# Expert stage of a one-core decoder step: token-transposed spreading inside the up product, a 20-unit weight ring, closing sums in PSUM

## The chip, the cores and the metric

The kernel runs on one core of a Trainium2 chip. The time is device time in microseconds (us) of one launch. Everything is float32. One execution was also taken by the hardware profiler; all durations below come from that one.

## What is computed

The kernel is one layer of a decoder for 256 prompt tokens and 8 sample tokens (264 rows of width 1024): sparse attention beside pooling groups, cross-attention into 256 memory tokens, and then a mixture of 32 experts, of which each token uses the 4 with the highest router score. Only that last part is changed:

```
logits  = tok @ router_w + router_b                 # (264, 32)
vals, idx = top_k(logits, 4);  gates = softmax(vals)
for each of 32 experts:
    h    = tok @ w_up[e] + b_up[e]                  # 1024 -> 2048
    gate = min(h[:, :1024], 7);  up = clip(h[:, 1024:], -7, 7)
    act  = gate * sigmoid(1.702 * gate) * (up + 1)
    acc += combine[:, e] * (act @ w_down[e] + b_down[e])   # 1024 -> 1024
y = rms_norm(h + acc) * norm_final
```

The weights of one expert are 8 MB (up) and 4 MB (down), so the 32 experts read 384 MB.

## The kernel before

**Layout.** The attention part keeps the residual h and the normalised tokens transposed, features on partitions and the 264 tokens along the row (`hT`, `xnT`: 8 blocks of 128 x 264). For the experts the kernel turns both back to tokens on partitions (`h_nat`, `xn_nat`, tiles of 128, 128 and 8 tokens; the `hn` transposes, L957, and the multiplication at L1687).

**One expert** works on 64 slots. VectorE writes a 0/1 matrix `slot_of` that says which token sits in which slot (`assign_slots`, L1740 to L1746). TensorE then does, in this order (`expert`, from L1035 on):

1. up product: 8 chunks (`unit(0..7)`, 1 MB each: 128 rows of 8 KB), four matmuls of 512 columns a chunk, in pairs side by side in two column halves of the array (L1042), into the banks `psh0`, `psh1`;
2. `gather_tokens` for the next expert (L1006): `slot_of` times `xn_nat`, two tiles of 128 tokens and one of 8, into `psx`;
3. `spread_rows` of the previous expert's output (L1029), in three parts r = 0, 1, 2, one a token tile: the turned slot matrix `ST` times `outb`, two matmuls of 512 columns, side by side in two row halves. VectorE adds each part, times the gate, into `h_nat` (L1754); a part waits until the part before is added (`y_added`);
4. between those parts: three transposes of the slot matrix (L1052), `up_bias` for the next expert (L1016, four matmuls with 32 rows), the four transposes of the gathered tokens (L1023) and of the activations (L1063);
5. down product: 4 chunks (`unit(8..11)`), L1075, into `pso`.

When the up product is full, VectorE clips gate and up (L1762, L1763), multiplies (L1766), ScalarE has computed the sigmoid (L1303), and VectorE multiplies again (L1769); when the down product is full it copies it to `outb` (L1780). ScalarE copies PSUM to SBUF for the transposes (L1283, L1287, L1306, L1309).

**Weights.** SyncE's queue issues all weight loads, in program order (L494 up, L499 down). There are 12 units of 1 MB. Chunk c of expert n+1 is loaded as soon as chunk c of expert n has been read (`chunk_free`). Before expert 0, the 12 chunks of expert 0 are loaded: 8 when cross-attention has freed their memory, 4 after the `mo` product. All queues are in order, and every engine counts semaphores; nothing is planned at run time but the list of experts, which the router part writes (two experts to a loop iteration).

**End.** After the last expert, three more `spread_rows`, each waiting for VectorE's add; then for each token tile ScalarE squares and sums (L1318) and takes the root (L1321), VectorE normalises (L1801), and SyncE stores.

Of the kernel before, what the change touches and what calls it, by code (L numbers as in the profile page):

```python
# [18 lines left out]
ALU = mybir.AluOpType  # L19
ACT = mybir.ActivationFunctionType  # L20
F32 = mybir.dt.float32
# [38 lines left out]
def shape_constants():  # L60
# [47 lines left out]
    c["iota64"] = np.tile(p % 64, (P, 1))  # L108
# [37 lines left out]
def psum_jobs():  # L146
# [44 lines left out]
    js += [("hn", r, g) for r in range(3) for g in range(2)]  # L191
    js += [("rsn",), ("rl",), ("pos",), ("gT",), ("item",)]
# [3 lines left out]
def build(nc, ins, outs, consts, ybuf):  # L196
# [6 lines left out]
    with ExitStack() as ctx:  # L203
# [61 lines left out]
        group_at["late"] = top[0]  # L265
        UT = misc(4, 16 + NT)
        assert width["late"] <= 4 * (16 + NT)
# [13 lines left out]
        un = at(temp_off + 2 * NT, 512)  # L281
        QB = misc(TS, 32)
# [9 lines left out]
        top8 = misc(8)  # L292
        vflat = misc(512)
        pnew = misc(2, P)
        stat = misc(64)
# [38 lines left out]
        u12 = 12 * UNIT  # L334
        h_nat = at(u12, 3, D)
        xn_nat = at(u12 + 3072, 3, D)
        gain_ffn = at(u12 + 6144, D)
        gain_fin = at(u12 + 7168, D)
        xe = at(u12 + 8192, 512)
        xeT = at(u12 + 8704, 4, P)  # L340
        actT = at(u12 + 9216, 4, P)
        gate_b = at(u12 + 9728, 512)
        sig_b = at(u12 + 10240, 512)
        act_b = at(u12 + 10752, 512)
        outb = at(u12 + 11264, 512)
        slot_of = [at(u12 + 11776, 3, P), at(qT_off, 3, P)]
        ST = [at(qT_off + 384, 3 * P), at(qT_off + 768, 3 * P)]
        ysq = at(4 * UNIT, 3, D)
        ybias = at(qiT_off, D)
        esel = [at(qiT_off + 1024, SLOTS), at(qiT_off + 1088, SLOTS)]  # L350
        posb = at(qiT_off + 1152, 3)
        gsc = at(qiT_off + 1156, 3)
        meta = at(qiT_off + 1160, 3, 2, NE)
        base = at(qiT_off + 1352, LIST)
        item_x = at(qiT_off + 1416, LIST)
        item_e = at(qiT_off + 1480, LIST).bitcast(I32)
        n_items = at(qiT_off + 1544, 1).bitcast(I32)
        n_pairs = at(qiT_off + 1545, 1).bitcast(I32)
        cur = [at(qiT_off + 1546, 3), at(qiT_off + 1549, 3)]
# [11 lines left out]

        pw_sb = misc(4, P)
        rw_sb = misc(KD, NE)
        rb_sb = misc(NE)

        banks = [ctx.enter_context(nc.psum_tensor(f"bank{b}", [P, 512], F32)) for b in range(8)]
# [70 lines left out]
        def _(sp):  # L447
# [31 lines left out]
            for g in range(4):  # L479
                wait_drained(sp, "pw", g)  # L480
# [6 lines left out]
            load(gain_ffn, norm_ffn.to_broadcast([P, D]), "gain_ffn_in")  # L487
            load(gain_fin, norm_final.rearrange("(o d) -> o d", o=1).to_broadcast([P, D]), "gain_fin_in")

            def load_expert(e, chunk):  # L490
                u = unit(chunk, UNIT)
                if chunk < 8:
                    src = w_up[0, bass.ds(e, 1), chunk * P:(chunk + 1) * P, :].rearrange("o p n -> p (o n)")
                    sp.dma_start(u, src).then_inc(S(f"chunk{chunk}_in"), 16)  # L494
                else:
                    j = chunk - 8
                    src = w_down[0, bass.ds(e, 1), 2 * j * P:2 * (j + 1) * P, :].rearrange(
                        "o (k p) n -> p (o k) n", p=P)
                    sp.dma_start(u.rearrange("p (k n) -> p k n", k=2), src).then_inc(S(f"chunk{chunk}_in"), 16)  # L499

            for chunk in range(4, 12):
                load_expert(0, chunk)
            wait_filled(sp, "mo", 7)
            for chunk in range(4):
                load_expert(0, chunk)
# [6 lines left out]
            def chunk_free(chunk, n):  # L512

                if chunk == 7:
                    sp.wait_ge(S("up_full"), n + 1)
                elif chunk == 11:
                    sp.wait_ge(S("down_full"), n + 1)
                else:
                    sp.wait_ge(S("chunk_read"), n * 10 + (chunk + 1 if chunk < 7 else chunk))

            for chunk in range(12):
                chunk_free(chunk, 0)
                load_expert(1, chunk)
            sp.wait_ge(S("list_ready"), 3)

            pairs = sp.value_load(n_pairs[0:1, :], min_val=NE // 2, max_val=LIST // 2 - 2)
            with sp.Fori(0, pairs - 1) as j:
                for b in range(2):
                    e = sp.value_load(item_e[0:1, bass.ds(j * 2 + 2 + b, 1)], min_val=0, max_val=NE - 1)
                    for chunk in range(12):  # L530
                        chunk_free(chunk, j * 2 + 1 + b)
                        load_expert(e, chunk)

            for r in range(3):
                sp.wait_ge(S("y_ready"), r + 1)
                dst = y_prompt[0, r * P:(r + 1) * P, :] if r < 2 else y_sample.rearrange("b s d -> (b s) d")
                sp.dma_start(dst, h_nat[0:ROWS[r], r, :]).then_inc(S("stored_y"), 16)
# [5 lines left out]
        def _(pool):  # L543
# [33 lines left out]
            for b in range(2):  # L577
                pool.memset(ST[b], 0.0).then_inc(S("st_zero"), 1)
# [6 lines left out]
        def _(pe):  # L585
# [366 lines left out]
            for r in range(3):  # L952
                for g in range(2):
                    b = take(pe, "hn", r, g)
                    for i in range(4):
                        k = 4 * g + i
                        ins = pe.transpose(b[0:ROWS[r], i * P:(i + 1) * P], hT[:, k, r * P:r * P + ROWS[r]], ident)  # L957
                    done(ins, "hn", r, g)
            b = take(pe, "rsn")
            pe.wait_ge(S("rstd_ready"), 3)  # L960
            for r in range(3):
                ins = pe.transpose(b[0:ROWS[r], r * P:(r + 1) * P], temp[:, 2, r * P:r * P + ROWS[r]], ident)
            done(ins, "rsn")
# [7 lines left out]
            done(ins, "rl")  # L971

# [27 lines left out]
            def gather_tokens(b, nth):  # L1000

                pe.wait_ge(S("slots_ready"), nth)
                for r in range(3):
                    w = ROWS[r]
                    for o in range(2):
                        ins = pe.matmul(psx[64 * o:64 * o + 64, :], slot_of[b][0:w, r, 64 * o:64 * o + 64],  # L1006
                                        xn_nat[0:w, r, o * 512:(o + 1) * 512], start=(r == 0), stop=(r == 2),
                                        skip_group_check=True)
                ins.then_inc(S("xe_full"), 1)

            def up_bias(b):

                for o in range(2):
                    for g, ps in enumerate((psh0, psh1)):
                        rows = slice(32 + 32 * g, 64 + 32 * g)
                        pe.matmul(ps[64 * o:64 * o + 64, :], esel[b][rows, :], ybias[rows, o * 512:(o + 1) * 512],  # L1016
                                  start=True, stop=False, skip_group_check=True)

# [7 lines left out]
            def spread_rows(b, r):  # L1026

                for o, ps in enumerate((psy0, psy1)):
                    ins = pe.matmul(ps[:, :], ST[b][64 * o:64 * o + 64, r * P:(r + 1) * P], outb[64 * o:64 * o + 64, :],  # L1029
                                    start=True, stop=True)  # L1030
                ins.then_inc(S("y_full"), 1)

# [801 lines left out]
```

## Time and profile before

| | us |
|---|---|
| three runs | 1430.21, 1431.46, 1432.88 (median 1431.46) |
| the profiled execution | 1439.72 |
| its span, first to last instruction | 1437.5 |
| TensorE busy | 1282.2 (89%) |
| VectorE busy | 486.9 (34%) |
| ScalarE busy | 213.7 (15%) |
| memory read in the span | 449.24 MB |

Busy times overlap between engines. The chain is the sequence of work, each piece released by the one before, that ended last. A row `64*128 64x512` is a matmul with 64 rows of the array, 128 columns of it, and 512 columns streamed; a float32 matmul leaves two records in the trace.

### The profile page before, as it was taken

The numbers are of one execution on the slowest core, as the hardware profiler recorded it, in microseconds if no ns is written. First come the engines' busy times: TensorE is split into PE (matmuls) and PEld (weight loads), VectorE is DVE, ScalarE is ACT, GpSimd is POOL, SyncE is SP. The second block draws the span as 40 slices with busy tenths as digits, with TensorE's granted clock in tenths as the row PEclk, the third lists the DMA queues.
The fourth block names the chain that finished last, engine by engine and source line by source line (L and its number), as shares of the span: only waits on it lengthen the run. The fifth ranks groups of instructions, "written<-read, shape, count | busy, mean of one in ns | idle before, by whom it ended". The sixth has DMA issues, their size and how long they took to land.

```text
span 1437.5 us, 16965 instructions
## 1 busy us (share of the span) xinstructions
PE 1282.2 (89%) x6251; PEld 572.7 (40%) x6251; DVE 486.9 (34%) x1057; ACT 213.7 (15%) x387; POOL 39.4 (3%) x46
## 2 busy tenths in 40 slices
PE   5997663897967999999999999999999999999996
PEld 3864532885652333333333333333333333333331
DVE  2358358202343322233322233322333222332224
ACT  2124231101321101011010111101111010110102
POOL 1012400000000000000000000000000000000000
PEclk9999775589977999999999999999999999999997
DMA  9303430333274999999999999999999999999980
GB/s 377 98 23 146 170 123 1 118 125 117 99 293 188 375 403 417 415 414 417 412 415 413 414 417 414 414 412 414 415 416 415 412 417 411 417 414 413 415 357 30
DMA packets 88088, 451.99 MB, mean 314 GB/s; under 512 B 8540, under 2 KB 9080, under 8 KB 53751
## 3 DMA queue, kind: packets, MB, share of 16 engines
q1 hardware_dynamic: 85631, 437.76, 75.3%
q0 software_dynamic: 2432, 13.89, 2.6%
q8 instruction: 17, 0.28, 0.1%
q14 instruction: 8, 0.07, 0.0%
HBM read 449.24 MB, written 2.61 MB: 314 GB/s over the span
## 4 chain that ended last, share of the span: by engine, by line
PE 82%; DVE 11%; issue 3%; ACT 2%; DMA 1%; POOL 1%; another core or an unknown queue 0%; SPq 0%; DVEq 0%; ACTq 0%
PE bank L1042 31%; PE bank L1075 16%; PE bank L1029 8%; PE bank L1006 6%; PE bank L629 4%; PE bank L1016 2%; PE bank L859 2%; DVE mem L1754 2%; PE bank L844 2%; PE bank L1023 1%; DVE mem L1555 1%; PE bank L868 1%; PE bank L1052 1%; PE bank L948 1%; PE bank L608 1%
## 5 line engine op out<-in xcount | busy, mean ns | idle before, releaser
L1042 PE MATMUL bank<-mem 128*64 128x512 f32 x2048 | 446.6, 594 | 0.8 <-ACT mem L1287 0.8
L1042 PEld LDWEIGHTS bank<-mem 128*64 128x64 f32 x2048 | 147.7, 137 | 293.8 <-issue 293.8
L1075 PE MATMUL bank<-mem 128*64 128x512 f32 x1024 | 226.8, 595 | 0.0
L1754 DVE SCALAR_TENSOR_TENSOR mem<-bank,mem 128x512 f32<-128x512 f32 (+1 forms) x198 | 139.1, 742 | 132.8 <-PE bank L1029 132.8
L1762 DVE TENSOR_SCALAR mem<-bank 128x512 f32<-128x512 f32 x32 | 22.1, 692 | 425.7 <-PE bank L1042 425.7
L1029 PE MATMUL bank<-mem 64*128 64x512 f32 x396 | 113.7, 651 | 33.4 <-DVE mem L1754 32.6
L1075 PEld LDWEIGHTS bank<-mem 128*64 128x64 f32 x1024 | 70.8, 137 | 152.1 <-issue 152.1
L1303 ACT ACTIVATE mem<-mem 128x512 f32<-128x512 f32 x32 | 20.2, 631 | 706.7 <-DVE mem L1762 706.7
L1006 PE MATMUL bank<-mem 128*64 128x512 f32 (+1 forms) x396 | 97.2, 609 | 2.5 <-DVE mem L1746 2.5
L1104 ACT ACTIVATE mem<-bank 128x512 f32<-128x512 f32 (+8 forms) x119 | 59.9, 530 | 189.1 <-PE bank L629 55.2
L1029 PEld LDWEIGHTS bank<-mem 64*128 64x128 f32 x396 | 30.2, 187 | 75.6 <-DVE mem L1754 42.6
L629 PE MATMUL bank<-mem 128*128 128x264 f32 (+1 forms) x224 | 53.9, 398 | 6.3 <-DVE mem L1343 6.3
L1780 DVE COPY mem<-bank 128x512 f32<-128x512 f32 x32 | 22.1, 692 | 95.6 <-PE bank L1075 95.6
L1006 PEld LDWEIGHTS bank<-mem 128*64 128x64 f32 (+1 forms) x396 | 25.6, 136 | 68.0 <-issue 68.0
L629 PEld LDWEIGHTS bank<-mem 128*128 128x128 f32 (+1 forms) x224 | 42.5, 191 | 16.2 <-DVE mem L1343 6.5
L712 PE MATMUL bank<-mem 128*128 128x128 f32 x128 | 21.9, 346 | 17.3 <-POOL mem L566 8.1
L1016 PE MATMUL bank<-mem 32*64 32x512 f32 x264 | 35.9, 613 | 0.0
L859 PE MATMUL bank<-mem 128*128 128x264 f32 x128 | 31.6, 413 | 0.5 <-DVE mem L1602 0.5
L859 PEld LDWEIGHTS bank<-mem 128*128 128x128 f32 x128 | 26.2, 206 | 5.6 <-DVE mem L1602 0.6
L844 PE MATMUL bank<-mem 128*64 128x8 f32 x256 | 27.4, 249 | 0.9 <-DVE mem L1597 0.9
L712 PEld LDWEIGHTS bank<-mem 128*128 128x128 f32 x128 | 20.2, 184 | 19.1 <-issue 8.8
L687 PE MATMUL bank<-mem 128*128 128x512 f32 x64 | 27.7, 594 | 0.0
(293 smaller groups left out, 943.5 us busy)
## 6 DMA issues: line engine op xcount, KB each, us to landing
mem<-in_w_up_dram SPq DMA_DIRECT2D x256, 1024.0 KB, 12.3
mem<-in_w_down_dram SPq DMA_DIRECT2D x128, 1024.0 KB, 7.7
mem<-in_w_in_dram SPq DMA_DIRECT2D x8, 868.0 KB, 19.0
mem<-in_w_o_dram SPq DMA_DIRECT2D x1, 4096.0 KB, 12.8
mem<-in_cache_mem_k_dram SPq DMA_DIRECT2D x1, 4096.0 KB, 15.5
mem<-in_cache_mem_v_dram SPq DMA_DIRECT2D x1, 4096.0 KB, 15.6
mem<-in_w_mk_dram SPq DMA_DIRECT2D x1, 2048.0 KB, 29.3
mem<-in_w_mv_dram SPq DMA_DIRECT2D x1, 2048.0 KB, 35.6
```

The lines of the kernel that those rows point to most:

```text
L629: ins = pe.matmul(b[0:w, 0:NT], w_in_sb[k][:, m * P:m * P + w], xnT[:, k, :], start=(k == 0), stop=(k == KD - 1))
L687: ins = pe.matmul(b[:, :], memT[:, k, t * P:(t + 1) * P], w[:, k, :], start=(k == 0), stop=(k == KD - 1))
L712: ins = pe.transpose(b[:, j * P:(j + 1) * P], both[:, (4 * i + j) % 32, :], ident)
L844: pe.matmul(o, V2[:, n * NPG + pg, :], spT[:, s, pg, 32 * b4:32 * b4 + NH], start=(pg == 0), stop=False)
L859: ins = pe.matmul(b[:, 0:NT], w_o_sb[:, k, m * P:(m + 1) * P], mixT[:, k, :], start=(k == 0), stop=(k == KD - 1))
L1006: ins = pe.matmul(psx[64 * o:64 * o + 64, :], slot_of[b][0:w, r, 64 * o:64 * o + 64], xn_nat[0:w, r, o * 512:(o + 1) * 512], start=(r == 0 ...
L1016: pe.matmul(ps[64 * o:64 * o + 64, :], esel[b][rows, :], ybias[rows, o * 512:(o + 1) * 512], start=True, stop=False, skip_group_check=True)
L1029: ins = pe.matmul(ps[:, :], ST[b][64 * o:64 * o + 64, r * P:(r + 1) * P], outb[64 * o:64 * o + 64, :], start=True, stop=True)
L1042: ins = pe.matmul(ps[64 * o:64 * o + 64, :], lhs, w[:, g * 1024 + o * 512:g * 1024 + (o + 1) * 512], start=False, stop=(k == 7), skip_grou ...
L1075: ins = pe.matmul(pso[64 * o:64 * o + 64, :], lhs, w[:, kk, o * 512:(o + 1) * 512], start=(k == 0), stop=(k == 7), skip_group_check=True)
L1104: ins = act.activation(out, in_, ACT.Copy)
L1754: ins = dve.scalar_tensor_tensor(out=v, in0=ps[0:w, :], scalar=gsc[0:w, r:r + 1], in1=v, op0=ALU.mult, op1=ALU.add)
```

## The change

- The output of an expert is spread with tokens along the row: `outb` is the stationary operand and `ST` (64 slots x 264 tokens a half) streams. Four parts c = 0..3, each two matmuls of 264 columns for two blocks of 128 features, are put between the up product's chunks (after chunks 0, 1, 2 and 4). VectorE adds them into `hT`. The gate is already in `ST`: `gate_slots` writes slot matrix times gate (`gated`), and that is transposed.
- `h_nat`, the `hn` and `rsn` transposes and the multiplication at L1687 go. The normalised tokens are turned from `xnT` (`xr`, 24 transposes after the router product).
- 20 units: the up chunks have two sets (chunk c of experts n and n+2 share a unit), the down chunks one. Before the loop, all of expert 0 and the eight up chunks of expert 1 are loaded (14 chunks where 8 were issued at first, then 4 and 1, and 1 after the `xr` transposes). A chunk stays 128 rows of 8 KB (up).
- `gather_tokens` is split: the two tiles of 128 tokens after the up product, the 8 samples together with the biases. The gate half of the up product releases VectorE before the up half is complete (`gate_full`), and sigmoid times gate is computed first.
- The last two experts stand outside the loop. The last one multiplies `hT` by the identity into PSUM (`turn_residual`, 8 matmuls a token tile), its output is spread on top of that, and ScalarE and VectorE read the sums from PSUM.

```diff
-            def expert(b, n):
-                pe.wait_ge(S("xet_copied"), n + 1)
-                for k in range(8):
-                    ...
-                gather_tokens(1 - b, n + 2)
-                pe.wait_ge(S("rows_out"), n + 1)
-                pe.wait_ge(S("st_copied"), n + 1)
-                spread_rows(1 - b, 0)
-                ...
-                up_bias(1 - b)
-                turn_tokens(n + 2)
-                pe.wait_ge(S("y_added"), n * 3 + 1)
-                spread_rows(1 - b, 1)
-                ...
-                spread_rows(1 - b, 2)
+            def spread_rows(c):
+                for o, ps in enumerate((psy0, psy1)):
+                    ins = pe.matmul(ps[:, 0:NT], outb[64 * o:64 * o + 64, c * P:(c + 1) * P],
+                                    ST[64 * o:64 * o + 64, :], start=True, stop=True)
+                ins.then_inc(S("y_full"), 1)
+            def up_product(b, n):
+                pe.wait_ge(S("xet_copied"), n + 1)
+                for chunk in range(8):
+                    up_chunk(b, n, chunk)
+                    if chunk == 0:
+                        pe.wait_ge(S("rows_out"), n + 1)
+                        pe.wait_ge(S("st_copied"), n + 1)
+                        spread_rows(0)
+                    elif chunk in (1, 2, 4):
+                        c = (1, 2, 4).index(chunk) + 1
+                        pe.wait_ge(S("y_added"), n * 4 + c)
+                        spread_rows(c)
+            def expert(b, n):
+                up_product(b, n)
+                gather_prompts(n + 2)
+                pe.wait_ge(S("act_ready"), n + 1)
+                pe.wait_ge(S("st_copied"), n + 1)
+                turn_activations()
+                gather_samples_and_bias()
+                pe.wait_ge(S("actt_copied"), n + 1)
+                down_chunk(n, 0)
+                turn_tokens(n + 2)
+                down_chunk(n, 1)
+                turn_slots()
+                down_chunk(n, 2)
+                down_chunk(n, 3)
+            def last_expert(b, n):
+                up_product(b, n)
+                pe.wait_ge(S("act_ready"), n + 1)
+                turn_activations()
+                pe.wait_ge(S("y_added"), n * 4 + 4)
+                turn_residual(0)
+                pe.wait_ge(S("actt_copied"), n + 1)
+                down_chunk(n, 0)
+                turn_slots()
+                turn_residual(1)
+                down_chunk(n, 1)
+                turn_residual(2)
+                down_chunk(n, 2)
+                down_chunk(n, 3)
 ...
-            with sp.Fori(0, pairs - 1) as j:
+            with sp.Fori(0, loops) as j:
                 for b in range(2):
-                    e = ...item_e[j * 2 + 2 + b]
+                    e_up = ...item_e[j * 2 + 2 + b];  e_down = ...item_e[j * 2 + 1 + b]
                     for chunk in range(12):
-                        chunk_free(chunk, j * 2 + 1 + b)
-                        load_expert(e, chunk)
+                        chunk_read(chunk, j * 2 + b)
+                        load_expert(b, e_up if chunk < 8 else e_down, chunk)
```

## Rows read from the trace of the kernel before

**Rows 1.** The page: busy us (share of span, instructions); GB/s in 40 slices.
```profile
PE 1282.2 (89%) x6251; PEld 572.7 (40%) x6251; DVE 486.9 (34%) x1057; ACT 213.7 (15%) x387; POOL 39.4 (3%) x46
GB/s 377 98 23 146 170 123 1 118 125 117 99 293 188 375 403 417 415 414 417 412 415 413 414 417 414 414 412 414 415 416 415 412 417 411 417 414 413 415 357 30
```
**Rows 2.** The chain over one expert: start us, us, what, pieces.
```profile
508.45 13.73 PE bank L1042 x64
522.18 2.72 PE bank L1006 x12
524.90 1.06 PE bank L1029 x4
525.96 0.52 PE bank L1052 x3
526.49 1.02 PE bank L1016 x8
527.50 0.58 PE bank L1023 x4
528.09 1.08 PE bank L1029 x4
...
529.25 0.61 issue
529.87 0.75 DVE mem L1754
530.66 1.13 PE bank L1029 x4
531.79 7.02 PE bank L1075 x32
538.81 13.73 PE bank L1042 x64
```
**Rows 3.** Timeline after an up product: start, us, engine line op [idle before].
```profile
825.84 0.69 DVE L1762 TENSOR_SCALAR mem<-bank 128x512 f32<-128x512 f32 x1 [13.04 <-PE bank L1042]
826.57 0.63 ACT L1303 ACTIVATE mem<-mem 128x512 f32<-128x512 f32 x1 [21.64 <-DVE mem L1762]
827.97 0.69 DVE L1769 TENSOR_TENSOR mem<-mem 128x512 f32<-128x512 f32 x1
```
**Rows 4.** Timeline before expert 0: samples' gather and biases, second records.
```profile
443.10 0.59 PE L1006 MATMUL bank<-mem 8*64 8x512 f32 x2
443.11 0.61 PE L1016 MATMUL bank<-mem 32*64 32x512 f32 x4
```
**Rows 5.** Groups by line, 384 to 446 us: busy us, mean ns, idle before.
```profile
L948 PE MATMUL bank<-mem 128*128 128x264 f32 x64 | 14.5, 387 | 0.8 <-DVE mem L1652 0.8
```
**Rows 6.** Up chunks issued at 522.36, 552.72, 1190.31, 1220.66: KB, us to landing.
```profile
mem<-in_w_up_dram SPq DMA_DIRECT2D x1, 1024.0 KB, 15.1
mem<-in_w_up_dram SPq DMA_DIRECT2D x1, 1024.0 KB, 14.9
mem<-in_w_up_dram SPq DMA_DIRECT2D x1, 1024.0 KB, 14.8
mem<-in_w_up_dram SPq DMA_DIRECT2D x1, 1024.0 KB, 15.5
```
**Rows 7.** The chain at the start of expert 0.
```profile
445.81 15.65 PE bank L1042 x64
```
**Rows 8.** Timeline: first issues of expert 1's chunks, and VectorE's token multiplication.
```profile
449.39 12.44 SPq L494 DMA_DIRECT2D mem<-in_w_up_dram  x8
425.27 3.67 DVE L1687 SCALAR_TENSOR_TENSOR mem<-mem 128x1024 f32<-128x1024 f32 x3
```
**Rows 9.** Timeline of the end of the kernel.
```profile
1419.33 0.69 DVE L1780 COPY mem<-bank 128x512 f32<-128x512 f32 x1 [2.98 <-PE bank L1075]
1430.36 1.28 DVE L1801 SCALAR_TENSOR_TENSOR mem<-mem 128x1024 f32<-128x1024 f32 x1
1433.97 1.27 DVE L1801 SCALAR_TENSOR_TENSOR mem<-mem 8x1024 f32<-8x1024 f32 x1
```

More of the change, by code:

```diff
@@ L971, in _ @@
             done(ins, "rl")
+            for r in range(3):
+                for g in range(2):
+                    b = take(pe, "xr", r, g)
+                    for i in range(4):
+                        k = 4 * g + i
+                        ins = pe.transpose(b[0:ROWS[r], i * P:(i + 1) * P], xnT[:, k, r * P:r * P + ROWS[r]], ident)
+                    done(ins, "xr", r, g)
             b = take(pe, "pos")
@@ new lines, in up_chunk @@
+            def up_chunk(b, n, chunk):
+                pe.wait_ge(S(f"up{chunk}_in{b}"), n * 8 + (16 - 8 * b))
+                w = ring(b, chunk)
+                k = chunk
+                lhs = xeT[:, k % 4, 64 * (k // 4):64 * (k // 4) + 64]
+                for g, ps in enumerate((psh0, psh1)):
+                    for o in range(2):
+                        ins = pe.matmul(ps[64 * o:64 * o + 64, :], lhs, w[:, g * 1024 + o * 512:g * 1024 + (o + 1) * 512],
+                                        start=False, stop=(k == 7), skip_group_check=True)
+                    if k == 7 and g == 0:
+                        ins.then_inc(S("gate_full"), 1)
+                ins.then_inc(S("chunk_read" if k < 7 else "up_full"), 1)
@@ new lines, in _ @@
+            last_expert(1, loops * 2 + 1)
+            pe.wait_ge(S("rows_out"), loops * 2 + 3)
+            pe.wait_ge(S("st_copied"), loops * 2 + 3)
+            for ps, r in tiles:
+                w = ROWS[r]
+                for o in range(2):
+                    ins = pe.matmul(ps[0:w, o * 512:(o + 1) * 512], ST[64 * o:64 * o + 64, r * P:r * P + w],
+                                    outb[64 * o:64 * o + 64, :], start=False, stop=True, skip_group_check=True)
+                ins.then_inc(S("y_sum"), 1)
@@ new lines, in add_rows, with expert @@
+            def add_rows(n, c):
+                dve.wait_ge(S("y_full"), n * 4 + c + 1)
+                v = hT.rearrange("p (o c) t -> p c o t", o=2)[:, c]
+                ps = psum[:, 6 * 512:8 * 512].rearrange("p (o t) -> p o t", o=2)[:, :, 0:NT]
+                dve.tensor_tensor(v, v, ps, ALU.add).then_inc(S("y_added"), 1)
+            def expert(n, last):
+                if not last:
+                    e = dve.value_load(item_e[0:1, bass.ds(n + 2, 1)], min_val=0, max_val=NE - 1)
+                for c in range(4):
+                    add_rows(n, c)
+                dve.wait_ge(S("gate_full"), n + 1)
+                dve.tensor_scalar(gate_b, banks[3], 7.0, None, ALU.min).then_inc(S("gate_ready"), 1)
@@ L1779, in expert @@
+                if not last:
+                    dve.wait_ge(S("st_full"), n + 1)
+                    dve.wait_ge(S("xe_full"), n + 2)
+                    gate_slots()
+                    dve.wait_ge(S("gated_ready"), n + 2)
+                    assign_slots(n + 3, e)
                 dve.wait_ge(S("down_full"), n + 1)
-                dve.tensor_copy(outb, banks[5][:, :]).then_inc(S("rows_out"), 1)
+                dve.tensor_copy(outb, banks[5]).then_inc(S("rows_out"), 1)
             dve.wait_ge(S("list_ready"), 3)
-            dve.memset(gate_b, 0.0).then_inc(S("rows_out"), 1)
```

362 lines of the change are left out of this document (167 added, 195 removed).

## The prediction

> **What bounds the kernel now.** I read the page's busy shares and 40 slices first, then the chain of waits, then the timeline of one expert, then the landings of the weight loads. The page [rows 1] shows two resources near their limit for the whole second half: TensorE (89% of the span) and the DMA engines, which move 412 to 417 GB/s in slice after slice; VectorE (34%) and ScalarE (15%) are far from it. Which of the two sets the pace the chain says [rows 2]: from one up product to the next it runs 538.81 − 508.45 = 30.36 us, and it is TensorE work but for one hole, 0.61 + 0.75 us, where the last `spread_rows` part waits for VectorE to add the part before. No piece of it is a transfer. So the loop is bound by TensorE, with about 1 us of waiting in it.
>
> The DMA is only just behind. The last up chunk of one expert, issued at 522.36, landed after 15.1 us, at 537.5; the one an expert later at 552.72 + 14.9 = 567.6 [rows 6]. That is 30.1 us for 12 chunks, with work always queued: a chunk costs 2.51 us. Now and then it stumbles: 1190.31 + 14.8 = 1205.1 and 1220.66 + 15.5 = 1236.2 are 31.1 us apart. I count four such expert periods, of about 1 us extra each, in the 31 (near 630, 800, 1010 and 1220 us), so the DMA's own period is 30.1 + 4/31 ≈ 30.25 us. TensorE's 30.36 hides it with 0.1 us to spare. Whatever is taken out of TensorE's expert beyond that has to be carried by chunks that are already loaded, and the change loads 8 more before expert 0.
>
> **TensorE's time for one expert after the change.** From [rows 2], piece by piece.
> - Up product 13.73: 64 records, two side by side, so 32 steps of 0.429. Unchanged.
> - Four spreads. Today two matmuls of 512 columns take 1.06, where two steps are 0.86: 0.2 is the switch to another tile shape, weights in view and the last records running out. The down product after it takes 7.02 where 16 steps are 6.86, so a switch back costs about 0.05 plus the run-out 0.09. For 264 columns a step is 14.5/64 = 0.226 [rows 5]; two are 0.45. Each spread between two up chunks is then 0.09 + 0.10 + 0.45 + 0.09 + 0.05 = 0.77, four 3.1. Bounds: 0.45 each (nothing shown of a switch, 1.8 in all), and 1.2 each (today's 1.06 with 512 columns plus the way back, 4.8). I take 0.77, since every switch in rows 2 has that size.
> - `gather_prompts`: 4 of the 6 steps that fill 2.72, 1.72.
> - Wait for the activations. Today VectorE begins 0.2 after TensorE has passed on (825.84 against 825.62, where this expert's gather starts) and ends at 828.66, 3.0 after it [rows 3]. Now the gate half is released two steps (0.86) earlier: gate clip at −0.64 to 0.05, sigmoid (0.63) to 0.7, up clip 0.22 to 0.9, two multiplications of 0.69 to 2.35. TensorE resumes at 2.4, 0.6 after its gather has ended. Behind this new wait stand the activation transposes, biases and the down product; nothing else uses TensorE.
> - Activation transposes 0.58, as L1023.
> - Biases with samples. Before expert 0 the samples' gather and the biases have their second records at 443.10 and 443.11 [rows 4]: six matmuls side by side, in the time of four. So 1.02 + 0.05 for all; bounds 1.07 and 1.07 + 0.86 if they follow each other. I take 1.07, the very same instructions.
> - Down product 6.86 + 0.05, with token transposes (0.58 + 0.14) and slot transposes (0.52 + 0.14) inside: 8.3.
>
> Sum: 13.73 + 3.1 + 2.4 + 0.58 + 1.07 + 8.3 = 29.2 us, 1.2 below today. Bounds: 27.9 and 31.7.
>
> The Trainium skill speaks against the four insertions: *TensorEngine Tiling (Array Packing)*, section Tiling Modes, says that a change of tiling mode, not just of tile, drains TensorE. The trace agrees, about 0.2 us for going into a shape and 0.14 for leaving it. Counted in the order of the code, an expert goes from 9 changes of shape to 15.
>
> The covers: `rows_out` for spread 0 is ready 0.23 + 0.69 after the down product [rows 9], inside chunk 0's 1.72. Each add, about 0.75, has at least one whole chunk between two spreads (1.72, then 1.72, then 3.43). ScalarE's copies lie under biases and down chunks, 0.6 each. VectorE's slot work (2 to 3 us) starts when the slot transposes are done and has the 3.5 us of the last two down chunks; it would delay `outb` only if it took 1 us more. These I cost at nothing.
>
> **The DMA against it.** Let T be the start of expert 0. All 12 chunks of expert 0 and 8 of expert 1 are there. The first issue of the loop follows the first chunk read, T + 3.6 (449.39 − 445.81 [rows 7, 8], TensorE's clock being low there). 8 chunks occupy the DMA to T + 23.7; the first down unit comes free at T + 15.65 + 3.1 + 4.1 + 1.8 = T + 24.6, so 0.9 is lost once. From then on a queue is always there, and group k (8 up of expert k+2, 4 down of expert k+1) ends at T + 4.5 + 30.25(k+1), landing 2.4 later.
> TensorE's need: expert k+1's first down chunk at T + 1.9 + 29.2(k+1) + 16.8 + 4.1, where 1.9 is 15.65 − 13.73. It lands at T + 4.5 + 30.25k + 9 × 2.51 + 2.4. The reserve is 22.5 − 1.05k, about 1 less for the fourth down chunk: used up near k = 20. So I expect no wait for weights in the first twenty experts, at 29.2 each, and then PE held to 30.25 by the down chunks.
> The last landing before the end is that of expert 30's fourth down chunk: T + 4.5 + 907.5 + 2.4 = T + 914.4. TensorE then has that chunk's 1.7 and the last expert: up 16.8, wait 2.4, transposes 0.6, residual 2.3, down chunk 1.8, slots 0.7, residual 2.3, chunk 1.7, residual 2.3, two chunks 3.5 = 34.4. A residual part is 8 matmuls, 16 records, at 0.145 each (0.58/4, L1023). The down product ends at D = T + 950.5.
> By TensorE alone D would be T + 1.9 + 31 × 29.2 + 34.4 = T + 941.5. The later one holds; they meet at 29.5 us an expert.
>
> **The ends.** Before: D = 1419.1 = T + 973.3, and 18.4 us follow. After: copy to `outb` at D + 0.2, spreads at D + 1.0, ScalarE at D + 2.2, first normalisation at D + 4.2; the three are (1433.97 − 1430.36)/2 = 1.8 apart [rows 9]; the last starts at D + 7.8, takes 1.3, and the store 2.2 (from 1435.2 to the span's end): 11.3 us. What goes is the two waits for adds and the larger part of the squaring.
> T itself: the token multiplication (3.67 [rows 8]) goes, but while it ran TensorE made the positions that VectorE needs next, until about 428.9; so that wait takes its place. `memset` against `memset` and narrower slot matrices give 0.2. The `xr` transposes and their copies (6 of some 0.5) lie under the router's selection on VectorE. The 14 early chunks, 5 more and the biases (2 us) keep the DMA busy to about 437; TensorE needs the biases at about 442. 5 us of cover; if it went, T would move by what is missing. I take T = 445.6, bounds ±2.
>
> Span: 445.6 + 950.5 + 11.3 = 1407.4, against 1437.5: −30.1. The profiled execution would go from 1439.72 to 1409.6. It stands 8.3 us above the median of the runs; taking the difference as the same, 1431.46 − 30.1 = **1401.4 us**.
>
> **The rivals.**
> 1. *TensorE all the way*: without the stumbles, or with a faster DMA in runs that aren't profiled, weights never hold TensorE. D = T + 941.5, 9 less: 1392. For it: the profiled execution is 8.3 us above the runs, so something is slower in it. Against it: the DMA is full in every slice. The Trainium skill (*DMA: Bandwidth & Descriptors*, Where 436 GB/s comes from) names 435 GB/s as the port limit, which would be 28.9 us for an expert and would give this case; the trace shows no slice above 417.
> 2. *Dearer switches*: at 29.9 us an expert TensorE sets the pace: D = T + 1.9 + 926.9 + 34.4 = T + 963.2, 12.7 later than forecast: 1414. For it: 15 changes of shape where there were 9, priced from a few examples, none of them from an up chunk into a spread.
> 3. *Slower than before*: the spreads cost 1.2 each and biases and samples follow one another: 31.7 us. D = T + 1.9 + 982.7 + 36.1 = T + 1020.7; 1472. It decides from 30.3 us an expert, where 1.9 + 31 × 30.3 + 34.4 + 11.3 meets today's 991.7 (T the same): each spread would have to cost 1.05. Against it: rows 4 and the 264 columns of rows 5.
> 4. *The units buy nothing*: TensorE is held at 30.25 from the start. Then D = T + 1.9 + 31 × 30.25 + 34.4 = T + 974, −6: 1425. Against it: the reserve of 22.5 us.
>
> **How the numbers follow.** Forecast 50%, rival 1 23%, rival 2 14%, rival 4 4%, rival 3 6%, no change 3%. Range 1388 to 1415: from rival 1 with T and the expert 0.1 lower, to rival 2; outside it are most of rivals 3 and 4, the no-change case and a tail of rival 2. A measurement tells about 0.2% (2.9 us) from no change. Faster 91%, same 3%, slower 6%.
>
> **What would show it.** In the chain, up to about expert 20: 29.2 us from up product to up product; L1029's successor with steps of 0.2 us and 0.77 in all; 0.6 of waiting before the activation transposes; bias and sample records starting together. Then TensorE waiting for down chunks, periods of 30.1 to 30.3, DMA above 410 GB/s until some 50 us before the end, and a tail of 11 us. Wrong if the chain never shows a transfer (rival 1), if the period is above 29.5 (rival 2), or if such waits begin before expert 15.

## The result and the profile after

The changed kernel takes 1399.55 us (median of 1398.05 to 1400.57) against 1431.77 us (1430.21 to 1432.88) for the kernel before in the same runs: ratio 0.9775, interval 0.9758 to 0.9792, 32.2 us less. On another chip it was 0.9772 (0.9741 to 0.9804). The forecast was 1401.4 us, range 1388 to 1415.

The page of the changed kernel, the two rows that answer to [rows 1]:

```profile
PE 1258.8 (90%) x6400; PEld 557.8 (40%) x6400; DVE 451.9 (32%) x1038; ACT 211.2 (15%) x385; POOL 38.9 (3%) x45
...
GB/s 377 113 23 108 193 151 1 121 132 118 102 419 245 398 417 416 417 419 418 419 418 416 416 418 419 418 418 417 417 418 418 418 419 417 417 417 419 418 377 31
```

TensorE's share has hardly moved; a share of busy time shows nothing of this change. The DMA row does: 416 to 419 GB/s in every slice from 489 to 1327 us, where before it wandered between 411 and 417.

The chain over one expert of the changed kernel (start us, us, what, pieces), to be laid beside [rows 2]:

```profile
477.73 5.33 PE psum L1066 x24
483.08 0.55 DVE mem L1828
...
483.69 0.69 DVE mem L1831
484.40 0.70 DVE mem L1833
...
485.15 0.66 PE psum L1048 x4
485.81 0.59 PE psum L1024 x4
486.41 0.41 PE psum L1024 x4
486.84 1.87 PE psum L1080 x8
488.71 0.59 PE psum L1035 x4
489.30 1.87 PE psum L1080 x8
491.16 0.52 PE psum L1042 x3
491.69 3.58 PE psum L1080 x16
495.27 1.72 PE psum L1066 x8
496.99 0.65 PE psum L1054 x4
497.63 1.87 PE psum L1066 x8
...
502.66 3.58 PE psum L1066 x16
506.24 0.65 PE psum L1054 x4
506.89 5.32 PE psum L1066 x24
```

From 477.73 to 506.89 it is 29.16 us, against 30.36. L1066 is the up product, L1054 a spread: 0.65 of its own, and the chunk behind it takes 1.87 where it takes 1.72 without a switch, so 0.80 in all. The three DVE lines between 483.08 and 485.1 are the new wait for the activations, 2.1 us in all (the four prompt gathers, 1.7 us, lie beside it and are not in the chain, so TensorE stands idle for 0.4). L1080 is the down product. L1024 (the biases) with the samples' gather beside it takes 1.0.

The waits of TensorE for transfers, first in the stretch from 1010 to 1050 us (the stretch from 500 to 1010 us has no such row), then from 1150 to 1355 us (us in total, times, longest):

```profile
PEld psum L1080 <- DMA mem<-in_w_down_dram: 0.9, 1, 0.9
```
```profile
PEld psum L1080 <- DMA mem<-in_w_down_dram: 17.9, 24, 1.5
PE psum L1080 <- DMA mem<-in_w_down_dram: 4.3, 7, 0.6
```

Twenty experts (0 to 19) without a wait for weights, then down chunks that come late; the first wait, at 1047 us, is in the down product of expert 20. The chain says it from the other side: expert 30's fourth down chunk, then the up product of the last expert, and what follows it (D, the end of the last down product, is at 1385.4):

```profile
1325.26 23.57 DMA mem<-in_w_down_dram
...
1348.88 1.94 PE psum L1080 x8
1350.82 1.72 PE psum L1066 x8
...
1370.51 3.20 PE psum L1120 x16
...
1385.61 0.70 DVE mem L1842
...
1386.35 1.15 PE psum L1159 x4
...
1389.37 1.28 DVE mem L1866
```

The expert sums' transposes (L1120) run from 1370.2 to 1382.0, beside work ahead of D. Behind D stand one copy (L1842), one spread (L1159) into the same PSUM tile, and then three passes of L1866, which read PSUM where it stands.

### The profile page after: what moved, and what is told of

Read it like the earlier page. It is cut to its first block, busy times and chain, and to the rows that moved or that the text cites. A ratio compares the mean times of both kernels' runs of the same rounds, so it can differ in the third digit from the quotient of the medians.

```text
span 1396.5 us, 17221 instructions
## 1 busy us (share of the span) xinstructions
PE 1258.8 (90%) x6400; PEld 557.8 (40%) x6400; DVE 451.9 (32%) x1038; ACT 211.2 (15%) x385; POOL 38.9 (3%) x45
## 4 chain that ended last, share of the span: by engine, by line
PE 59%; SPq 21%; DVE 12%; issue 3%; DMA 3%; ACT 2%; POOL 1%; DVEq 0%; ACTq 0%
PE psum L1066 22%; SPq L508 12%; PE psum L1080 11%; SPq L504 8%; PE psum L1054 4%; PE psum L645 4%; PE psum L875 2%; PE psum L860 2%; DMA mem<-in_w_down_dram 2%; PE psum L1024 2%; DVE mem L1622 1%; PE psum L884 1%; PE psum L624 1%; DVE mem L1833 1%; DVE mem L1831 1%
## 5 line engine op out<-in xcount | busy, mean ns | idle before, releaser
L1066 PE MATMUL psum<-mem 128*64 128x512 f32 x2048 | 474.6, 600 | 0.8 <-ACT mem L1351 0.8
L1080 PE MATMUL psum<-mem 128*64 128x512 f32 x1024 | 243.5, 603 | 6.8 <-DMA mem<-in_w_down_dram 6.1
L1066 PEld LDWEIGHTS psum<-mem 128*64 128x64 f32 x2048 | 135.7, 137 | 264.4 <-issue 264.4
L1817 DVE TENSOR_TENSOR mem<-mem,psum 128x528 f32<-128x528 f32 x128 | 90.2, 704 | 285.5 <-PE psum L1054 285.5
L1080 PEld LDWEIGHTS psum<-mem 128*64 128x64 f32 x1024 | 64.0, 136 | 134.0 <-issue 106.2
L1054 PE MATMUL psum<-mem 64*128 64x264 f32 x512 | 91.8, 435 | 0.0
L1168 ACT ACTIVATE mem<-psum 128x512 f32<-128x512 f32 (+8 forms) x119 | 60.2, 530 | 194.5 <-PE psum L645 55.0
L1054 PEld LDWEIGHTS psum<-mem 64*128 64x128 f32 x512 | 38.7, 185 | 104.7 <-issue 104.7
L1016 PE MATMUL psum<-mem 128*64 128x512 f32 x256 | 62.2, 607 | 2.4 <-DVE mem L1801 2.4
L645 PE MATMUL psum<-mem 128*128 128x264 f32 (+1 forms) x224 | 53.8, 397 | 6.3 <-DVE mem L1410 6.3
L645 PEld LDWEIGHTS psum<-mem 128*128 128x128 f32 (+1 forms) x224 | 42.5, 191 | 16.1 <-DVE mem L1410 6.5
L1842 DVE COPY mem<-psum 128x512 f32<-128x512 f32 x32 | 22.2, 693 | 62.8 <-PE psum L1080 62.8
L728 PE MATMUL psum<-mem 128*128 128x128 f32 x128 | 20.1, 326 | 16.7 <-POOL mem L583 7.5
L1024 PE MATMUL psum<-mem 32*64 32x512 f32 x256 | 34.9, 615 | 0.0
L1016 PEld LDWEIGHTS psum<-mem 128*64 128x64 f32 x256 | 18.7, 140 | 39.2 <-issue 39.2
L1048 PE MATMUL psum<-mem 128*128 128x128 f32 x128 | 21.0, 287 | 14.7 <-DVE mem L1833 14.7
L875 PE MATMUL psum<-mem 128*128 128x264 f32 x128 | 30.1, 399 | 0.5 <-DVE mem L1669 0.5
```

The costliest lines, as they stand in the source:

```text
L645: ins = pe.matmul(b[0:w, 0:NT], w_in_sb[k][:, m * P:m * P + w], xnT[:, k, :], start=(k == 0), stop=(k == KD - 1))
L875: ins = pe.matmul(b[:, 0:NT], w_o_sb[:, k, m * P:(m + 1) * P], mixT[:, k, :], start=(k == 0), stop=(k == KD - 1))
L1016: pe.matmul(psx[64 * o:64 * o + 64, :], slot_of[:, r, :], xn01[:, r, o * 512:(o + 1) * 512], start=(r == 0), stop=False, skip_group_check= ...
L1024: pe.matmul(ps[64 * o:64 * o + 64, :], esel[rows, :], ybias[rows, o * 512:(o + 1) * 512], start=True, stop=False, skip_group_check=True)
L1054: ins = pe.matmul(ps[:, 0:NT], outb[64 * o:64 * o + 64, c * P:(c + 1) * P], ST[64 * o:64 * o + 64, :], start=True, stop=True)
L1066: ins = pe.matmul(ps[64 * o:64 * o + 64, :], lhs, w[:, g * 1024 + o * 512:g * 1024 + (o + 1) * 512], start=False, stop=(k == 7), skip_grou ...
```

## How the executions are compared

In each trace T is the start of expert 0 and D the end of the last down product (start of its last record + 0.43). An expert's time, its period, runs from the start of its up product to the start of the next. What TensorE does ahead of T is the same code but for the last 61 us (from the `mo` product on), and it varies by itself:

```
                T      D - T   after D   an expert, us (most / once weights hold TensorE)
before        445.8    973.3    18.4     30.36
before, again 450.4    973.3    18.4     30.36
after         435.1    950.3    11.1     29.16 / 30.12
after, again  449.8    951.0    11.1     29.16 / 30.12
b_pair        442.9    949.6    17.4     28.81 / 30.12
a_late1       443.8    964.3    11.1     29.16 / 30.12
a_half        437.5    940.3    11.1     29.16
a_onespread   438.2    943.9    11.1     26.77 / 30.1
a_together    442.9   1070.7    11.1     31.33, 33.0 and 34.19
a_hold        442.2    937.9    11.1     29.16
h_gatelate    442.8    972.5    11.1     30.01 (four of 31.66)
h_apart       441.1    954.7    11.1     29.67
h_fill        437.8    931.7    11.1     28.53 / 30.12
```

T moves by 15 us between executions of one kernel, D − T by 0.7 us or less. Expert 0 itself takes 29.2 to 31.2 us in kernels with a 29.16 us expert, by TensorE's clock at that moment; differences of up to 2 us in D − T come from there. The last expert has the same looseness. In the changed kernel the clock falls in it (granted 0.52 from 1370.5 to 1373.9 us), and the first residual part takes 3.20 us; in a_late1 and a_hold it does not fall, that part takes 1.79, and the last expert is 1.6 us shorter.

## The experiments

Each was timed in rounds with the kernel before; ratios are against it.

**b_again**: the kernel before, a second execution under the profiler.

> The kernel before, unchanged, for a second profile. Theory: the profiled execution of before was 8 us long because of the stages ahead of the expert stage, which both kernels share (from 177 us on the trace of after is 8 to 12 us ahead of it), so a second execution has its span at 1429 to 1430 us, expert 0 starting near 437 us, and again 30.36 us an expert and 18.4 us after the last down product. Rival: the change itself moved the start of expert 0 from 445.8 to 435.1 us; then this profile starts expert 0 at 445 to 446 us again.

The ratio was 1.0003 (0.9976 to 1.003), T 450.4, not 437. My theory that the first profiled execution had been an odd one fell; so does the rival, since the changed kernel, executed again, has T = 449.8. T is simply loose. What the change does to the stretch from the router product to T can still be read, because both ends lie close together: 33.4 to 33.5 us in three executions of the old code, 32.0 to 33.2 in ten of the new, mostly 32.5. Measured from the `mo` product, where the code begins to differ, it is 60.7 us in two of the three old ones and 59.7 to 59.9 in eight of the ten new ones. The chain at that place in the changed kernel, router product and start of expert 0:

```profile
403.09 7.97 PE psum L973 x48
...
435.08 3.43 PE psum L1066 x8
```

About 0.9 us, no more.

**b_pair**: the kernel before with another order of TensorE's work after the up product: the samples' gather goes beside the biases, and the token transposes go behind the second spread (ScalarE's two copies that follow them change places too).

```diff
-                for r in range(3):                       # gather_tokens, after the up product
+                for r in range(2):
 ...
                 up_bias(1 - b)                           # now with the 8 samples' two matmuls
-                turn_tokens(n + 2)
                 pe.wait_ge(S("y_added"), n * 3 + 1)
                 spread_rows(1 - b, 1)
+                turn_tokens(n + 2)
```

> The kernel before with one part of the change: the samples' gather beside the biases, and the second spread ahead of the token transposes. TensorE's expert should fall by 1.4 to 1.7 us, to about 28.8. Theory (two clocks: TensorE's, and 30.12 us of DMA for every expert once its queue is full): the last chunk lands at T + 3.6 + 3 + 31 x 30.12 + 2.4 = T + 943, one chunk's product later the last down product ends, T + 944.7 against T + 973.3 before: 28.6 us less, 1403 us. Rival 1, TensorE alone sets the time: 32 x 1.6 = 51 us less, 1380. Rival 2, the DMA already held the kernel before at 30.36 an expert: 8 us less at most, 1424.

1412.37 us (1412.16 to 1412.52), ratio 0.982 (0.9789 to 0.9851); D − T fell by 23.7 us, as much as with the whole change. The expert takes 28.81 us up to expert 11 (expert 0, at the lower clock, 30.56), and then 30.12, with 78 us of waits for up chunks. So rival 1 (51 us) and rival 2 (8 us) are out. The theory's 28.6 was 5 us too high. The last chunk lands at T + 942.9, where the theory had T + 943, but it is not what the end waits for: the chain's last transfer is the last *up* chunk, which lands at T + 932.75, and behind it stand 16.9 us of TensorE's own work, from that chunk's product (1375.70) to D. It also corrects something I had taken for granted: at 30.36 us an expert the kernel before was not about to be held by its DMA. Its last weights land 21.6 us before D, and that reserve could be spent.

**a_late1**: the change without the early loads of expert 1.

```diff
-            for chunk in range(6):
-                load_expert(1, 1, chunk)
 ...
-            load_expert(1, 1, 7)
 ...
-            load_expert(1, 1, 6)
+            sp.wait_ge(S("chunk_read"), 1)
+            for chunk in range(8):
+                load_expert(1, 1, chunk)
```

> The changed kernel without the early loads: the eight up chunks of expert 1 are issued only when expert 0's first chunk has been read. Theory (the DMA holds the last experts): 8 x 2.51 = 20 us more on the DMA's side, less about 1 us of idle time that they fill: 19 us more than the changed kernel, 1418.5, with TensorE waiting for weights from about expert 2 to 5 on. Rival (TensorE sets the time all through, the extra units buy nothing): within 2 us of 1399.5.

1422.14 us (1417.86 to 1430.9), ratio 0.9901 (0.9866 to 0.9936). Periods of 30.11 us from expert 3 on, D − T 964.3: 14.0 us more than the changed kernel where 19 were expected. The theory holds, and the landings show where the 5 us are. Expert 1's fourth down chunk lands at T + 55.8 here and T + 39.5 in the changed kernel, 16.3 later and not 20: eight chunks that stand ready keep the queue full, where the changed kernel's first issues come one by one and its DMA stands idle for 3.3 us in that cycle, and expert 0 runs at the higher clock here, so that the first issue comes 1.5 us earlier. The last expert at the higher clock gives 1.6 more.

**a_half**: half of each down chunk left out in the loop.

```diff
+                    if half:
+                        v, src = v[:, :, 0:512], src[:, :, 0:512]
```

> The changed kernel with half of each down chunk loaded in the loop (columns 0 to 511 of each row; the other half keeps what an earlier expert left there, so the result is not the reference's). TensorE's work is the same; the DMA's expert falls from 30.1 to about 25. Theory: TensorE's own time shows, T + 1.9 + 31 x 29.16 + 34.8 = T + 940.7 against T + 950.5, 9.8 us less: 1389.8, and no wait for a transfer. Rival (the DMA costs nothing in the changed kernel): within 2 us of 1399.5.

D − T 940.3 against an expected 940.7, no wait for a transfer, 30 periods of 29.16 after expert 0's 30.8 (1392.48 us, ratio 0.9705, 0.9658 to 0.9751). That is what the changed kernel would be if the DMA never held it; 10.0 us are lost there.

**a_onespread**: three of four spreads and adds left out.

```diff
-                    elif chunk in (1, 2, 4):
-                        c = (1, 2, 4).index(chunk) + 1
-                        pe.wait_ge(S("y_added"), n * 4 + c)
-                        spread_rows(c)
```

> The changed kernel with one spread of the four in each expert (the matmuls and adds of parts 1 to 3 are left out, so the result is not the reference's). TensorE's expert falls by 3 x 0.80 = 2.4 us, to 26.8. Theory (the DMA holds the end): the last landing moves by 1 to 2 us only, the last expert is 2.4 shorter: 3 to 5 us less than the changed kernel, about 1395.5, TensorE waiting for weights from about expert 6 on at 30.1 us an expert. Rival (TensorE sets the time): 32 x 2.4 = 77 us less, 1322.

TensorE's expert fell by 2.39 us (26.77), and D − T by 6.4, not 77 (1396.66 us, ratio 0.9736, 0.9697 to 0.9776). Of the 6.4, 4.0 are the last expert, 2.4 by its own spreads and 1.6 because the clock did not fall in it; the last down chunk of expert 30 lands only 2.4 earlier. From expert 7 on the average period is 30.1; single ones are 28.4 to 31.9, since TensorE now waits up to 3.4 us for a down chunk and its clock falls in 12 of them. Less work on TensorE buys nothing more here.

**a_together**: the four spreads directly behind one another.

```diff
                         spread_rows(0)
-                    elif chunk in (1, 2, 4):
-                        c = (1, 2, 4).index(chunk) + 1
-                        pe.wait_ge(S("y_added"), n * 4 + c)
-                        spread_rows(c)
+                        for c in range(1, 4):
+                            pe.wait_ge(S("y_added"), n * 4 + c)
+                            spread_rows(c)
```

> The changed kernel with all four spreads of an expert directly behind one another after chunk 0, each waiting for the add of the part before. Theory: a spread then comes every 1.45 us (0.65 of its own, 0.75 of add, starts) instead of 0.65, three times, and three changes of shape (0.15 each) are saved: 1.95 us more an expert, 31.1 us, above the DMA's 30.12, so all of it shows above 29.5: T + 1.9 + 31 x 31.1 + 36.8 = T + 1002.8, 52 us more, about 1452. Rival (the places between the chunks buy nothing, adds are hidden by the queue anyway): within 5 us of 1399.5.

1527.03 us, ratio 1.0634 (1.0597 to 1.0671): 120 us more in D − T where I expected 52. Seven of the 31 periods are 31.3 to 31.4, near the 31.1 expected, five are 33.0, and nineteen are 34.1 to 34.2. The windows (busy us by engine, granted clock, DMA share, GB/s) of the waiting stretch of such an expert, of the 8 us behind it, and of a 31.33 expert:

```profile
735.90:743.70 7.80, 5.39 (x26) 1.80 (x22) 2.80 (x4) 0.00 (x0) 0.00 (x0) 0.81 1.03 414
743.70:752.00 8.30, 8.30 (x32) 2.60 (x32) 0.70 (x1) 0.00 (x0) 0.00 (x0) 0.77 0.60 231
600.00:631.30 31.30, 28.47 (x145) 9.68 (x143) 8.25 (x20) 2.79 (x5) 0.00 (x0) 1.00 1.00 399
```

and the chain through it:

```profile
738.29 0.71 DVE mem L1816
...
739.05 0.74 PE psum L1054 x4
...
739.82 0.71 DVE mem L1816
...
740.57 1.12 PE psum L1054 x4
...
741.72 0.72 DVE mem L1816
...
742.47 1.25 PE psum L1054 x4
743.73 14.13 PE psum L1066 x56
```

After the second of three waits of 0.8 us TensorE's clock falls to its lower level (1.2 of 2.4 GHz) for a few us: the spread behind it takes 1.12 instead of 0.74, and the seven chunks take 14.13 where the expert whose up product starts at 603 us has 12.19. That is so in nineteen experts; in the five of 33.0 it falls after the third wait and costs 1.65, and in the seven of 31.3 not at all, although their waits are the same. The waits cost 2.2 us, the clock up to 2.9 more. The places between the chunks are therefore worth 120 us, not 52.

**a_hold**: another order of loads from expert 18 on.

```diff
-                    for chunk in range(12):
+                    for chunk in order:      # (0..11) for 9 iterations, then
 ...                                          # (0, 1, 2, 3, 8, 9, 10, 11, 4, 5, 6, 7)
```

> The changed kernel with another order of the loads from expert 18 on: up chunks 4 to 7 of expert n+2 are issued after the four down chunks of expert n+1. Theory (TensorE waits only for down chunks that stand behind ten up chunks in the queue, while the up chunks come a whole expert early): the down chunks land 10 us earlier, more than the 12 x 0.96 us by which the DMA falls behind until the end, TensorE never waits: T + 940.7, 9.8 us less, 1389.8. Rival 1 (the DMA's total is what counts, the order nothing): within 2 us of 1399.5. Rival 2 (the queue runs dry at the new order): slower.

1392.19 us (1391.14 to 1401.87), ratio 0.9704 (0.9671 to 0.9737). D − T 937.9, 12.4 us less than the changed kernel, of which 1.6 is expert 0's clock and 1.6 the last expert's: the order itself gives about 9.2 (9.8 expected). All periods are 29.16 but expert 0's and the last, 29.96. The waits left for transfers:

```profile
PEld psum L1086 <- DMA mem<-in_w_down_dram: 3.2, 5, 1.5
PE psum L1086 <- DMA mem<-in_w_down_dram: 0.6, 1, 0.6
```

Both rivals are out. The DMA moves the same bytes at the same rate; what counted was which chunk stood in front.

**h_gatelate** and **h_apart**, both on top of a_hold, where TensorE's time is visible.

```diff
-                dve.wait_ge(S("gate_full"), n + 1)       # h_gatelate
+                dve.wait_ge(S("up_full"), n + 1)
                 dve.tensor_scalar(gate_b, banks[3], 7.0, None, ALU.min)
```

> The reordered loads (a_hold, where TensorE sets the time) with VectorE's gate clip released by the whole up product again, not by its gate half. Theory: gate clip at 0.22 to 0.9 after the up product, sigmoid to 1.6, two multiplications to 3.05, TensorE resumes 0.7 us later in each expert: 29.85 us an expert, 32 x 0.7 = 22 us more than a_hold from the start of expert 0 to the last down product (T + 937.9 there, 960 here). Rival (the up clip and the sigmoid hide it): below 3 us.

```diff
                                   start=(r == 0), stop=False, ...)     # h_apart: end of gather_prompts
+                for o in range(2):
+                    ins = pe.matmul(psx[64 * o:64 * o + 64, :], slot_of[0:TS, 2, :],
+                                    etab[0:TS, o * 512:(o + 1) * 512], start=False, stop=True, ...)
```

> The reordered loads (a_hold) with the samples' gather directly after the prompts' again, not beside the biases. Theory: alone it takes 1.0 us, of which 0.6 falls into the wait for the activations: TensorE resumes at 2.75 instead of 2.4 us after the up product, and the biases keep their 1.0: 0.35 us more an expert, 11 us in all (T + 949). Rival 1 (pairing is worth nothing, they overlap anyway): 0. Rival 2 (its full 0.86 to 1.0 shows): 27 to 32 us.

h_gatelate: 1427.45 us, ratio 0.9932 (0.9911 to 0.9952), an expert 30.01, 0.85 more than a_hold (0.7 expected), D − T 34.6 more (22 expected). Four periods of 31.66 add 6.6 of that, and they are the clock's: in the first, 472.9 to 504.5 us, it is granted at 0.55 from 494.6 to 498.1, in the expert behind it at 1.00 all the way. The last expert's clock falls too (1.4). The early release of the gate half is worth about 27 us, and it keeps the clock up. The chain after its up product has the sigmoid back between the gate clip and the multiplications:

```profile
703.43 0.70 DVE mem L1832
...
704.16 0.64 ACT mem L1373
...
704.89 0.70 DVE mem L1837
...
705.62 0.70 DVE mem L1839
```

h_apart (VectorE's gating of the slot matrix, which waited for the samples' gather, now waits for the biases): 1409.5 us, ratio 0.9812 (0.9784 to 0.9841), an expert 29.67, 0.51 more (0.35 expected); D − T 16.8 more (11 expected), 1.6 of it the last expert's clock. In its chain the samples take a 1.00 of their own:

```profile
725.28 1.72 PE psum L1022 x8
727.00 1.00 PE psum L1025 x4
728.00 0.59 PE psum L1055 x4
728.59 1.02 PE psum L1034 x8
```

728.59 to 729.6 is 1.02 for the biases alone, and they took 1.0 with the samples beside them above: pairing is free. Without it half of the samples' 1.0 is hidden in the wait for the activations, and the other half shows.

**h_fill**: the fourth spread moved into the wait for the activations, six up chunks behind the down chunks.

```diff
                 up_product(b, n)                          # spreads after chunks 0, 2, 4
                 gather_prompts(n + 2)
+                pe.wait_ge(S("y_added"), n * 4 + 3)
+                spread_rows(3)
```

> The changed kernel with the fourth spread moved from the up product into the wait for the activations, and from expert 18 on six up chunks (2 to 7) issued behind the down chunks. Theory: TensorE's expert falls by the 0.80 us of one spread, its wait goes: 28.4 us; TensorE alone T + 918; the DMA then sets the end: expert 30's down chunks land 6 x 2.51 = 15 us before the T + 913.8 of the changed kernel, T + 934.5 in all, 15.8 less than the changed kernel's T + 950.3, about 3.5 less than a_hold's. Rival 1 (the wait is TensorE's own by another name, the spread shows there): 29.16 an expert, as a_hold. Rival 2 (the queue runs dry when six chunks are held back): above a_hold.

1387.02 us (1382.64 to 1393.3), ratio 0.9665 (0.9639 to 0.9691), D − T 931.7 (934.5 expected), 18.6 less than the changed kernel and the best here; 1.6 of it is the last expert's clock. The expert takes 28.53 (28.4 expected), and the chain has no DVE piece any more: VectorE has the activations ready before the spread (L1060) ends.

```profile
707.20 5.30 PE psum L1072 x24
712.50 1.72 PE psum L1022 x8
714.22 0.65 PE psum L1060 x4
714.86 0.59 PE psum L1054 x4
```

The DMA then holds it at 30.12 in experts 13 to 18 and at the end (36 us of waits for down chunks): the DMA is the bound again.

**a_again**: the changed kernel once more, for T and D − T.

> The changed kernel, unchanged, on the chip of these runs. Theory: from the start of expert 0 (T) to the last down product again 950 us, less up to 1.7 if TensorE's clock is up in expert 0; T itself moves by several us from execution to execution in the stages that are not changed (435 to 450 us so far), which is why the comparison with a_hold and h_fill goes by T + x. Rival (the 950.3 was one execution's luck): outside 948 to 951.

1404.92 us (1398.95 to 1414.02); T 449.8, D − T 951.0, expert 0 at 31.24. The theory holds, though barely: 951.0 stands at the very edge of the 948 to 951 outside which the rival began, and the slower expert 0 explains only 0.4 of the 0.7 more.

## Why the prediction was right, step by step

The mechanism was right: TensorE alone for twenty experts, then the down chunks at the DMA's pace. That D − T came out within 0.2 us was luck, since errors of 1.4 to 3 us cancelled in two places (the DMA's own time, and the last expert).

- *What bounds the loop*: TensorE, with the DMA close behind. Right (b_pair, a_half, a_onespread each show one side).
- *TensorE's expert*: 29.2 forecast, 29.16 measured. The parts: a spread 0.77, measured 0.80; wait to the activations 2.4 after the up product, measured 2.1; activation transposes 0.58, measured 0.66; biases with samples 1.07, measured 1.0; down product with both transposes 8.3, measured 8.43 (486.84 to 495.27). *TensorEngine Tiling (Array Packing)* of the Trainium skill, Tiling Modes, is borne out again: each excursion of a spread costs 0.35 us beyond the 0.45 of streaming.
- *Where the weights begin to hold TensorE*: forecast expert 20, measured first at 1047 us, in expert 20's down product.
- *The DMA's own period*: mis-sized. I took 30.25, with four stumbles of 1 us. With a full queue it is 30.12 in after, b_pair and a_late1, and no stumble is seen. The kernel before does not show the DMA's own pace at all: from expert 1 to expert 31 its down chunks land 30.36 us apart on average, which is TensorE's period, in steps of 30.1 to 31.1. Its queue ran nearly dry in each expert (a down chunk issued at T + 57.7 finds only one load left, which lands at T + 61.0), and the next issue came barely in time ([rows 6]: 14.8 and then 15.5 for the same chunk). A resource that seems busy all the time with odd slow periods may just be fed late. From expert 1's fourth down chunk to expert 30's I forecast 877.3 us, and measured are 874.3.
- *The first cycle*: forecast 0.9 us of idle DMA. The twelve landings from T + 8.6 to T + 39.5 take 30.9 us where eleven steps of 2.51 are 27.6, so it was 3.3. Expert 1's fourth down chunk was forecast at T + 37.2 and landed at T + 39.5. This and the line above nearly cancel. Last landing: forecast T + 914.4, measured T + 913.8.
- *The last expert*: 34.4 from its up product to D, measured 34.6 (1350.82 to 1385.4). At the higher clock it is 33.0 (a_late1, a_hold): the residual parts take 1.8 to 2.0 us there, not 2.3. That the clock fell in this execution and in a_again was no part of the forecast, and made up for it. D − T: forecast 950.5, measured 950.3.
- *The ends*: 11.3 after D, measured 11.1. No run takes the closing sums out alone; that they give 7.3 us is read from the two chains. T: forecast −0.2, measured about −0.9.
- *The sum*: −23.0 (D − T), −7.3 (after D), −0.9 (T) are −31.2 us of the 32.2 between the medians; the forecast had −22.8, −7.1, −0.2. The remaining 1 us is within the looseness of T. That looseness hit the forecast for the profiled execution itself: 1409.6 was forecast and 1398.58 came, since T was 435.1 and not 445.6. The 8.3 us between the profiled execution of before and the runs were probably T's too, since D − T and the end are the same in both of its traces; the runs without a trace cannot show it.
- *Rivals*. 1 (TensorE all the way) is what a_half shows with fewer bytes: 10 us better, not the case. The 435 GB/s of the Trainium skill (*DMA: Bandwidth & Descriptors*, Where 436 GB/s comes from) is not reached by 4 and 8 KB rows here: 419 at most in a slice of the page. 2 and 3 fall with the 0.80 of a spread, 4 with nineteen periods of 29.16 behind expert 0. In rival 3 a sum was off: 1.9 + 31 × 30.3 + 34.4 + 11.3 is 986.9, not 991.7; the break-even lies near 30.4 us an expert.
- What I had not seen: the greater part of the gain did not need the ring. b_pair has the same D − T with a few lines moved, and its expert is the shorter one, 28.81 against 29.16. In the changed kernel, the spreads inside the up product and the ring together leave TensorE at 29.16 with weights that last longer; without the early loads the change is worth 9.0 us in D − T (a_late1).

## What to carry to other kernels

When two resources run within 1% of each other, write both as a line over the experts (start, period, reserve), and ask of every saving which line it moves; the end is the later of the two. When transfers set the pace, look at the order in the queue before the bytes: a transfer that is needed next should not stand behind ones that are needed an expert later. And fill TensorE's short waits with work that is due anyway: a wait costs its length, and several close together, or a single one of 1 to 2 us, can also cost the clock.

## What the runs showed of the hardware

- TensorE's clock fell from 2.4 to 1.2 GHz for a few us (granted 0.81 and 0.77 in the two stretches shown) after two or three waits of 0.8 us each for VectorE, in 24 of 31 periods of a_together. With one wait of 1.2 us an expert it fell in 4 of 31 (h_gatelate). After the one wait of 2.1 us in the last expert it fell in the changed kernel and not in a_hold. In the experts before the last of a_hold, with one wait of 0.4 us each, it never fell. The same wait can thus cost the clock or not; what decides it, these runs do not show.
- SyncE's issue of a load takes long when many loads are under way: up to 6.2 us. The same instruction has these durations (min/median/max ns), in the kernel before and in the changed one:

```profile
L499 SPq DMA_DIRECT2D mem<-in_w_down_dram x128: 368/382/3727, 388.0 to 1389.1; - x128
```
```profile
L508 SPq DMA_DIRECT2D mem<-in_w_down_dram x128: 372/469/6170, 376.2 to 1351.0; - x128
```

The chain of the changed kernel puts 21% of the span on SyncE (12% on L508, 8% on L504) for this reason: followed back from a late landing it finds a long issue. That the issue waits for room in the queue is my reading, not shown by itself; a_half speaks for it, where the bytes are fewer, the median issue of L512 takes 378 ns, and SyncE has 0% of the chain.
- Two float32 matmuls of 8 rows beside four of 32 rows cost nothing (1.0 us for six, 1.02 for the four alone in h_apart).
